# Cached memory keys and values of the sample group as plain fp32 products of 32 columns, with a ring of ten slots

## The chip, the cores and the metric

The kernel runs on one core of one Trainium2 chip. The metric is the device time of one execution in microseconds (us), as the median of several runs. The engines named below are TensorE (PE, with its weight loads PEld), VectorE (DVE), ScalarE (ACT), GpSimd (POOL) and SyncE (SP), which here only issues DMAs.

## The reference, cut to what matters

A two-layer decoder trunk is evaluated for a prompt of 512 tokens and, with the same weights, for a sample group of 8 sequences of 4 tokens. In each layer both groups attend to 256 memory tokens with 4 heads of width 256. The prompt's memory keys and values are computed in the kernel; those of the sample group come from caches, one set for each of its 8 sequences:

```python
def memory_attend(h, mem_k, mem_v, w, layer):
    bsz, seq, _ = h.shape
    q = rms_norm((h @ w['mem_w_q'][layer]).reshape(bsz, seq, MEM_HEADS, MEM_HD), w['mem_q_norm'][layer])
    s = jnp.einsum('blhd,bmhd->bhlm', q, mem_k.astype(q.dtype)).astype(jnp.float32) * MEM_HD ** -0.5
    p = jax.nn.softmax(s, axis=-1).astype(mem_v.dtype)
    o = jnp.einsum('bhlm,bmhd->blhd', p, mem_v).reshape(bsz, seq, D_MODEL)
    return o.astype(h.dtype) @ w['mem_w_o'][layer]
```

For the sample group `mem_k` and `mem_v` are `cache_mem_k[layer]` and `cache_mem_v[layer]`: 8 x 256 x 1024 fp32 numbers each, 8.4 MB each for a layer.

## The kernel before

All matrix products of large size are made in three passes of F32R operands: every operand is split into a high part, rounded to F32R by ACT, and a low part, the remainder, made by DVE, and PE adds up high by high, high by low and low by high (`PASSES`). `projection` (line 100) does so with streamed weights: SP loads chunks of 512 KB, ACT makes `w_high` (line 92), DVE makes `w_low` (line 96), PE multiplies (line 305).

`memory_attention` (line 938) runs once in each of the two layers. It makes the prompt's keys and values, then, in a block called `ring`, loads the first cached keys and clears two buffers `own_high` and `own_low`; then come the query projection (with the weight pair of the output projection loaded at its end), the norm of the queries, the block `attend`, and the output projection. All engines meet at the end of each block.

**The sample group in `attend`.** The caches come as 16 items for a layer: items 0 to 7 are the keys of the eight sequences, items 8 to 15 their values. An item is 1 MB and arrives as two halves of 512 KB, [128, 1024] fp32, in the slots of `ring`, which has 6 (`load`, line 1004). For each half ACT makes `ring_high` (line 1314) and DVE makes `ring_low` (line 1243), in buffers of three slots (`PARTS`). The four query columns of the sequence and of each head lie in `own_high` and `own_low`, which hold zeros elsewhere, so that a window of 128 columns of them puts that sequence and head at its own 4 of 128 output rows; all products of the eight keys add up in one PSUM bank (`half_item`, line 1143). A half item has 4 tiles of three passes, each product 128 x 128 by 128 x 256 (line 1157). After item 7 the scores of all sequences and heads stand in that bank and go through one softmax (stage "sample"), are turned and are used with the values in the same way.

**The prompt in `attend`.** Four heads, each with the stages: `scores` on PE (24 products, line 1113), `shift` on DVE (a maximum and a subtraction over [128, 1024], lines 1205 and 1210), `exps` on ACT (line 1285), `divide` on DVE (a sum, a reciprocal of [128, 4] and a product, lines 1215, 1217 and 1219), `turn` on PE (8 transposes, line 1127), `turned_copy` on ACT (line 1291), `turned_low` on DVE (line 1223), `values` on PE (12 products with 512 columns, line 1138), `high` on ACT (line 1297, two pieces) and `low` on DVE (line 1230, two pieces). `scores` of a head waits for the `shift` of the head before it.

**What sets the order.** Each engine has one stream of instructions, written out by hand. On PE it is: scores 0, item 0, scores 1, item 1, turn 0, item 2, scores 2, values 0, item 3, turn 1, scores 3, values 1, item 4, turn 2, item 5, values 2, item 6, turn 3, item 7, values 3, turn of the sample group, items 8 to 15, and two transposes of the result (line 1190). DVE and ACT have the parts of the items (`low_parts`, `high_parts`) between their softmax steps. SP issues the load of half j once the low part of half j - 6 is made. A half that is not split yet stops PE, and an item that PE has not used yet stops ACT:

```python
act.wait_ge(ring_in[j % RING], 16 * (j // RING + 1))
if j >= PARTS:
    act.wait_ge(used, j - PARTS + 1)
...
pe.wait_ge(split_low, j + 1)
```

**Elsewhere.** The second layer's state-space stage (`s5`, "chunked": the prompt in pieces) has plain fp32 products with a stationary operand of 128 x 32, whose outputs go to 32 PSUM rows each, four in turn (lines 1439 and 1572). The norms use plain fp32 products of 128 x 128 by 128 x 272 (line 389), and the sliding-window attention those of 64 x 128 by 64 x 256 (line 1820). In the profile a plain fp32 product stands as two matmul records, an F32R product as one.

## Time and profile before

| what | value |
|---|---|
| runs | 3186.57, 3183.14, 3183.83 us; median 3183.83 |
| profiled execution | 3189.84 us, of which its span is 3187.9 us |
| PE busy in the span | 2785.0 us (87%) |
| DVE, ACT, POOL busy | 1393.0 us (44%), 964.7 us (30%), 163.2 us (5%) |
| granted TensorE clock, mean | 0.910 |
| DMA | 258.87 MB, mean 81 GB/s |
| loads of `mem_ring` | 64 of 512 KB, median 4.6 us from issue to landing |
| products of line 1157, both layers | 3 kinds x 256, 78.5, 76.4 and 76.2 us busy |
| low parts of the ring (line 1243) | 64, 76.7 us busy on DVE |
| high parts of the ring (line 1314) | 64, 66.6 us busy on ACT |

Busy times of one engine overlap those of others. A matmul's duration is from its start to its modelled end; products that follow each other overlap, so their cost is the distance between starts. The granted clock is given as a share of 2.4 GHz; it has two levels, 1.0 and 0.5 (1.2 GHz), and a mean between them says how long each held. The profiled execution is 6.0 us longer than the median of the runs.

### The profile page before, as it was taken

To read this page: it belongs to the slowest core of one execution; us is meant where nothing else is said; L and a number is where in the kernel's file an instruction comes from. 1 tells how busy PE (TensorE), PEld (TensorE's weight loads), DVE (VectorE), ACT (ScalarE), POOL (GpSimd) and SP (SyncE) were. 2 spreads that over 40 slices of the span, in tenths; PEclk is the share of its full clock that TensorE was granted. 3 is DMA by queue.
4 is the path that set the end of the run, shared out by engine and by line. 5 is a ranking of instruction groups with operands and counts; after the bars stand their busy time and mean duration, and the time that the engine had idled before them with its cause. 6 is when DMAs were issued, how large, how long until landed. Compare 5 with 4: busy or idle time off the path is not lost. (4 is left out here: it accounts for less than half of the span.)

```text
span 3187.9 us, 50690 instructions
## 1 busy us (share of the span) xinstructions
PE 2785.0 (87%) x20835; PEld 2659.6 (83%) x20835; DVE 1393.0 (44%) x1888; ACT 964.7 (30%) x1249; POOL 163.2 (5%) x139
## 2 busy tenths in 40 slices
PE   6999989778586688999989999988698678899998
PEld 6999989757576688999989999986357568899998
DVE  5424433242344554434436334246543547443342
ACT  4412221210434443412224212132432444342221
POOL 0000000000000000000018000050000000000000
PEclk9999999865788899999999999999559889999999
DMA  3222222210133242222222222220103414222222
GB/s 112 96 69 92 94 65 86 81 27 22 49 120 119 66 146 68 90 86 79 89 76 90 93 75 92 73 67 23 38 20 99 139 60 146 77 86 94 73 90 83
DMA packets 76359, 258.87 MB, mean 81 GB/s; under 512 B 9780, under 2 KB 19204, under 8 KB 75232
## 3 DMA queue, kind: packets, MB, share of 16 engines
q1 hardware_dynamic: 75728, 255.81, 24.9%
q0 software_dynamic: 528, 1.64, 0.2%
q8 instruction: 71, 1.16, 0.2%
q14 instruction: 32, 0.26, 0.0%
HBM read 246.85 MB, written 10.57 MB: 81 GB/s over the span
## 5 line engine op out<-in xcount | busy, mean ns | idle before, releaser
L96 DVE TENSOR_TENSOR w_low<-w_raw,w_high 128x1024 fp32r<-128x1024 f32 (+2 forms) x360 | 470.7, 1307 | 1274.6 <-ACT w_high L92 1274.3
L305 PE MATMUL ps<-h_high,w_high 128*128 128x272 f32 x4192 | 887.1, 293 | 124.0 <-DVE h_low L254 67.5
L305 PE MATMUL ps<-h_high,w_low 128*128 128x272 f32 x4192 | 879.1, 292 | 0.0
L305 PE MATMUL ps<-h_low,w_high 128*128 128x272 f32 x4192 | 877.7, 291 | 0.0
L92 ACT ACTIVATE w_high<-w_raw 128x1024 fp32r<-128x1024 f32 (+2 forms) x360 | 399.6, 1111 | 1440.5 <-PE ps L305 1332.9
L305 PEld LDWEIGHTS ps<-h_high,w_high 128*128 128x128 f32 x4192 | 673.4, 192 | 132.0 <-DVE h_low L254 70.5
L305 PEld LDWEIGHTS ps<-h_low,w_high 128*128 128x128 f32 x4192 | 673.0, 193 | 0.0
L305 PEld LDWEIGHTS ps<-h_high,w_low 128*128 128x128 f32 x4192 | 667.2, 192 | 0.0
L305 PE MATMUL ps<-ffn_hid,w_high 128*128 128x272 f32 x2816 | 473.2, 290 | 24.7 <-PEq L149 24.7
L305 PEld LDWEIGHTS ps<-ffn_hid,w_high 128*128 128x128 f32 x2816 | 401.5, 190 | 26.2 <-issue 26.2
L305 PE MATMUL ps<-ffn_hid,w_low 128*128 128x272 f32 x1408 | 294.0, 290 | 0.0
L305 PEld LDWEIGHTS ps<-ffn_hid,w_low 128*128 128x128 f32 x1408 | 222.7, 190 | 0.0
L305 PE MATMUL ps<-mem_mh,w_high 128*128 128x256 f32 x512 | 102.0, 301 | 27.9 <-DVE mem_mh L254 18.1
L305 PEld LDWEIGHTS ps<-mem_mh,w_high 128*128 128x128 f32 x512 | 85.3, 205 | 31.6 <-DVE mem_mh L254 19.1
L1157 PE MATMUL ps<-mem_ring_high,mem_own_high 128*128 128x256 f32 x256 | 78.5, 306 | 22.9 <-DVE mem_ring_low L1243 22.9
L244 DVE SCALAR_TENSOR_TENSOR x<-ps,x 128x544 f32 (+1 forms) x96 | 69.1, 719 | 60.8 <-PE ps L305 60.8
L190 ACT ACTIVATE ffn_up_sg<-ffn_up_sg 128x544 f32<-128x544 f32 x88 | 58.0, 659 | 123.8 <-DVE ffn_up_sg L228 123.8
L1243 DVE TENSOR_TENSOR mem_ring_low<-mem_ring,mem_ring_high 128x1024 fp32r<-128x1024 f32 x64 | 76.7, 1221 | 9.9 <-ACT mem_ring_high L1314 9.5
L1314 ACT ACTIVATE mem_ring_high<-mem_ring 128x1024 fp32r<-128x1024 f32 x64 | 66.6, 1051 | 37.4 <-PE ps L1157 37.4
L1157 PE MATMUL ps<-mem_ring_low,mem_own_high 128*128 128x256 f32 x256 | 76.4, 298 | 0.0
L1157 PE MATMUL ps<-mem_ring_high,mem_own_low 128*128 128x256 f32 x256 | 76.2, 298 | 0.0
L305 PE MATMUL ps<-mem_mh,w_low 128*128 128x256 f32 x256 | 75.5, 295 | 0.0
(379 smaller groups left out, 2476.4 us busy)
## 6 DMA issues: line engine op xcount, KB each, us to landing
w_raw<-in_ffn_w_gate SPq DMA_DIRECT2D x88, 512.0 KB, 3.5
w_raw<-in_ffn_w_up SPq DMA_DIRECT2D x88, 512.0 KB, 3.5
w_raw<-in_ffn_w_down SPq DMA_DIRECT2D x64, 704.0 KB, 4.0
mem_ring<-in_cache_mem_k SPq DMA_DIRECT2D x32, 512.0 KB, 4.6
mem_ring<-in_cache_mem_v SPq DMA_DIRECT2D x32, 512.0 KB, 4.6
w_raw<-in_even_w_in SPq DMA_DIRECT2D x26, 512.0 KB, 3.5
w_raw<-in_mem_w_k SPq DMA_DIRECT2D x16, 512.0 KB, 3.6
w_raw<-in_mem_w_v SPq DMA_DIRECT2D x16, 512.0 KB, 3.5
```

Of the source, the lines that this page charges most:

```text
L92: return nc.scalar.activation(core.high[s][:, 0:kt * P], core.raw[s][:, 0:kt * P], ACT.Copy)
L96: return nc.vector.tensor_tensor(core.low[s][:, 0:kt * P], core.raw[s][:, 0:kt * P], core.high[s][:, 0:kt * P].bitcast(F32), ALU.subtract)
L190: nc.scalar.activation(sg[:], sg[:], ACT.Silu).then_inc(gate_ready, 1)
L244: ins = nc.vector.scalar_tensor_tensor(out, acc[s], scale, out, ALU.mult, ALU.add)
L305: last = nc.tensor.matmul(acc[s][:, a, :], w, x[:, k, a * width:(a + 1) * width], start=(k == 0 and n == 0), stop=(k == kt - 1 and n == 2))
L1157: ins = nc.tensor.matmul(core.ps[:, 6, 0:N_MEM], own[mine][:, i % 2, first:first + P], (ring_high, ring_low)[streamed][:, j % PARTS, at:at ...
L1243: nc.vector.tensor_tensor(ring_low[:, j % PARTS], ring[:, j % RING], ring_high[:, j % PARTS].bitcast(F32), ALU.subtract).then_inc(split_lo ...
L1314: nc.scalar.activation(ring_high[:, j % PARTS], ring[:, j % RING], ACT.Copy).then_inc(split_high, 1)
```

## The change

The sample group's parts are not split any more. An item is 8 plain fp32 products on the fp32 ring itself, each with a stationary operand of 32 columns (the 8 x 4 sample columns of one head, where only the item's own sequence is not zero) and 256 moving columns, and its result goes to the 32 PSUM rows of its head. DVE's and ACT's parts of the items fall away (`low_parts`, `high_parts`), and with them `ring_high`, `ring_low`, `own_high` and `own_low`. In their place are `own_q`, made by one DVE sum of the queries' high and low parts, and `own_p`, made by one ACT copy of the turned probabilities; both are cleared by POOL beforehand, [128, 2048] each.

The ring has 10 slots. Six halves are loaded where six were loaded before; four more are issued by SP in the query projection, behind the first weight chunk that it loads (`fetch`). In `attend` SP issues both halves of item i once PE has used item i - 5. PE waits for the two landings of an item itself, and for `own_q` or `own_p` ahead of item 0 or 8. The order of the steps on PE is as before; line numbers from there on are 2 to 40 less.

```diff
-def projection(nc, core, name, weights, pairs, kt, src, cols, finish, dst, scale=1.0, after=None, norm=None, scaled=False, beside=None):
+def projection(nc, core, name, weights, pairs, kt, src, cols, finish, dst, scale=1.0, after=None, norm=None, scaled=False, beside=None, fetch=None):
...
                 load(0, weights[0][1], kt)
+                if fetch is not None:
+                    fetch(sp)
...
-        RING, PARTS = 6, 3
+        RING, EARLY = 10, 6
         HALF = KT * N_MEM // 2
-        HALVES = 4 * DEC_BATCH
+        ITEMS = 2 * DEC_BATCH
...
-        FRONT = DEC_SEQ * (DEC_BATCH - 1)
-        own = [sb("own_high", [P, 2, FRONT + KT * P], F32R), sb("own_low", [P, 2, FRONT + KT * P], F32R)]
-        zeros = core.mats[:, IDENT, 0:1].unsqueeze(2).broadcast_to([P, 2, FRONT + KT * P])
+        own_q = sb("own_q", [P, KT, DEC_BATCH, TS])
...
         with nc.Block(f"{name}_ring") as block:
             @block.sync
             def _(sp):
-                for j in range(RING):
+                for j in range(EARLY):
                     load(sp, j)
-            @block.scalar
-            def _(act):
-                nc.scalar.activation(own[0][:], zeros, ACT.Copy, scale=0.0)
-            @block.vector
-            def _(dve):
-                nc.vector.tensor_scalar(own[1][:], zeros, 0.0, None, ALU.mult)
+            @block.gpsimd
+            def _(pool):
+                nc.gpsimd.memset(own_q[:], 0.0)
+        def load_more(sp):
+            for j in range(EARLY, RING):
+                load(sp, j)
...
-                   norm=of_x(core, VEC["mem_x_norm"] + KT * layer), scaled=True)
+                   norm=of_x(core, VEC["mem_x_norm"] + KT * layer), scaled=True, fetch=load_more)
...
-        ring_high = sb("ring_high", [P, PARTS, HALF], F32R)
-        ring_low = sb("ring_low", [P, PARTS, HALF], F32R)
+        own_p = sb("own_p", [P, 2, MEM_HEADS, DEC_BATCH, TS])
...
+                @block.gpsimd
+                def _(pool):
+                    nc.gpsimd.memset(own_p[:], 0.0).then_inc(own_cleared, 1)
...
-                    for j in range(RING, HALVES):
-                        sp.wait_ge(split_low, j - RING + 1)
+                    for j in range(RING, 2 * ITEMS):
+                        if j % 2 == 0:
+                            sp.wait_ge(used, (j - RING) // 2 + 1)
                         load(sp, j)
...
-                    def half_item(j):
-                        i, m = j // 2, j % 2
+                    def item(i):
                         b = i % DEC_BATCH
-                        pe.wait_ge(split_low, j + 1)
-                        if i < DEC_BATCH:
-                            tiles = [(h, t, (2 * (h - 2 * m) + t) * N_MEM) for h in (2 * m, 2 * m + 1) for t in range(2)]
-                        else:
-                            tiles = [(h, m, 2 * h * P) for h in range(MEM_HEADS)]
-                        for h, t, at in tiles:
-                            first = FRONT + (2 * h + t) * P - h * TS - b * DEC_SEQ
-                            for n, (mine, streamed) in enumerate(PASSES):
-                                start = b + m + n == 0 and (h, t, at) == tiles[0]
-                                stop = b == DEC_BATCH - 1 and m == 1 and n == 2 and (h, t, at) == tiles[-1]
-                                ins = nc.tensor.matmul(core.ps[:, 6, 0:N_MEM], own[mine][:, i % 2, first:first + P],
-                                                       (ring_high, ring_low)[streamed][:, j % PARTS, at:at + N_MEM],
-                                                       start=start, stop=stop)
+                        for j in (2 * i, 2 * i + 1):
+                            pe.wait_ge(ring_in[j % RING], 16 * (j // RING + 1))
+                        if i == 0:
+                            pe.wait_ge(queries_ready, 1)
+                        elif i == DEC_BATCH:
+                            pe.wait_ge(sample_turned, 1)
+                        for t in range(2):
+                            for h in range(MEM_HEADS):
+                                if i < DEC_BATCH:
+                                    mine = own_q[:, 2 * h + t, b, :]
+                                    part, at = h // 2, (2 * (h % 2) + t) * N_MEM
+                                else:
+                                    mine = own_p[:, t, h, b, :]
+                                    part, at = t, 2 * h * P
+                                ins = nc.tensor.matmul(core.ps[h * TS:(h + 1) * TS, 6, 0:N_MEM], mine,
+                                                       ring[:, (2 * i + part) % RING, at:at + N_MEM],
+                                                       start=(b == 0 and t == 0), stop=(b == DEC_BATCH - 1 and t == 1))
                         ins.then_inc(used, 1)
...
-                    def low_parts(first, count):
-                        for j in range(2 * first, 2 * (first + count)):
-                            i = j // 2
-                            dve.wait_ge(split_high, j + 1)
-                            if j % 2 == 0 and i < DEC_BATCH:
-                                nc.vector.tensor_copy(own_columns(1, i), sample_queries(1, i).bitcast(F32))
-                            elif j % 2 == 0:
-                                nc.vector.tensor_tensor(own_columns(1, i), sample_probs(i),
-                                                        own_columns(0, i).bitcast(F32), ALU.subtract)
-                            nc.vector.tensor_tensor(ring_low[:, j % PARTS], ring[:, j % RING],
-                                                    ring_high[:, j % PARTS].bitcast(F32), ALU.subtract
-                                                    ).then_inc(split_low, 1)
-                    low_parts(0, 1)
+                    sample = [core.h[part][:, :, SEQ:TOK].rearrange("p f (b c) -> p f b c", c=DEC_SEQ) for part in range(2)]
+                    nc.vector.tensor_tensor(own_columns(own_q), sample[0].bitcast(F32), sample[1].bitcast(F32), ALU.add
+                                            ).then_inc(queries_ready, 1)
                     shift(0)
-                    low_parts(1, 1)
...
-                    def high_parts(first, count):
-                        for j in range(2 * first, 2 * (first + count)):
-                            i = j // 2
-                            act.wait_ge(ring_in[j % RING], 16 * (j // RING + 1))
-                            if j >= PARTS:
-                                act.wait_ge(used, j - PARTS + 1)
...
-                            if j % 2 == 0:
-                                source = sample_queries(0, i).bitcast(F32) if i < DEC_BATCH else sample_probs(i)
-                                nc.scalar.activation(own_columns(0, i), source, ACT.Copy)
-                            nc.scalar.activation(ring_high[:, j % PARTS], ring[:, j % RING], ACT.Copy
-                                                 ).then_inc(split_high, 1)
-                    high_parts(0, 1)
-                    high_parts(1, 1)
...
+                    act.wait_ge(turned, NS)
+                    act.wait_ge(own_cleared, 1)
+                    nc.scalar.activation(own_columns(own_p.rearrange("p t h b c -> p (t h) b c")),
+                                         core.ps[:, 7, N_MEM:2 * N_MEM].rearrange("p (f b c) -> p f b c", f=KT, c=DEC_SEQ),
+                                         ACT.Copy).then_inc(sample_turned, 1)
```

PE in `attend`, first layer, at scores 0 and item 0. Before (the last three products of the scores and the first three of the item's 24):

```order
L1113 MATMUL ps<-mem_k_high,h_high 128x256
L1113 MATMUL ps<-mem_k_low,h_high 128x256
L1113 MATMUL ps<-mem_k_high,h_low 128x256
L1157 MATMUL ps<-mem_ring_high,mem_own_high 128x256
L1157 MATMUL ps<-mem_ring_low,mem_own_high 128x256
L1157 MATMUL ps<-mem_ring_high,mem_own_low 128x256
```

After, the same place (the numbers are partitions or columns of the stationary operand by moving columns):

```order
L1108 MATMUL ps<-mem_k_high,h_high 128x256
L1108 MATMUL ps<-mem_k_low,h_high 128x256
L1108 MATMUL ps<-mem_k_high,h_low 128x256
L1155 MATMUL ps<-mem_ring,mem_own_q 32x256 x8
L1108 MATMUL ps<-mem_k_high,h_high 128x256
```

The item's 24 products became 8, between the same scores.

DVE at the start of `attend`, first layer. Before:

```order
L1239 CAST mem_own_low<-h_low 128x8x4
L1243 TENSOR_TENSOR mem_ring_low<-mem_ring,mem_ring_high 128x1024 x2
L1205 TENSOR_REDUCE rstd<-ps 128x4
L1210 TENSOR_TENSOR mem_prob<-ps,rstd 128x1024
L1239 CAST mem_own_low<-h_low 128x8x4
L1243 TENSOR_TENSOR mem_ring_low<-mem_ring,mem_ring_high 128x1024 x2
L1215 TENSOR_REDUCE rstd<-mem_prob 128x4
```

After:

```order
L1233 TENSOR_TENSOR mem_own_q<-h_high,h_low 128x8x8x4
L1203 TENSOR_REDUCE rstd<-ps 128x4
L1208 TENSOR_TENSOR mem_prob<-ps,rstd 128x1024
L1213 TENSOR_REDUCE rstd<-mem_prob 128x4
L1215 RECIPROCAL rstd<-rstd 128x4
L1217 TENSOR_TENSOR mem_prob<-mem_prob,rstd 128x1024
L1203 TENSOR_REDUCE rstd<-ps 128x4
```

The softmax steps now follow each other on DVE; ACT has lost its parts in the same way.

SP from the block `ring` into the query projection, first layer (the weights of the query projection are `mem_w_q`). Before:

```order
L1009 DMA mem_ring<-in_cache_mem_k 128x1024 x6
L1018 UNCONDITIONAL_BRANCH
L150 UNCONDITIONAL_BRANCH
L153 DMA w_raw<-in_mem_w_q 128x1024
L157 UNCONDITIONAL_BRANCH
L157 ISA
```

After:

```order
L1011 DMA mem_ring<-in_cache_mem_k 128x1024 x6
L1024 UNCONDITIONAL_BRANCH
L150 UNCONDITIONAL_BRANCH
L153 DMA w_raw<-in_mem_w_q 128x1024
L1011 DMA mem_ring<-in_cache_mem_k 128x1024 x4
L159 UNCONDITIONAL_BRANCH
```

Four loads moved from `attend` to the query projection, ahead of the weight chunks that follow the first.

## Rows read from the trace of the kernel before

**Rows 1.** Stretches of both attend blocks: us, busy by engine, PEclk, DMA share, GB/s.

```profile
1077.30:1146.20 68.90, 55.45 (x370) 51.22 (x370) 51.75 (x64) 32.25 (x47) 0.00 (x0) 0.92 0.38 122
1146.20:1171.20 25.00, 24.94 (x192) 24.63 (x192) 18.88 (x22) 15.15 (x20) 0.00 (x0) 0.93 0.63 211
...
2610.80:2679.80 69.00, 56.34 (x370) 52.51 (x370) 51.79 (x64) 32.37 (x47) 0.00 (x0) 0.90 0.38 122
2679.80:2706.00 26.20, 26.10 (x192) 25.75 (x192) 18.89 (x23) 15.12 (x20) 0.00 (x0) 0.88 0.60 201
```

**Rows 2.** Groups by line, first attend block: count | busy us, mean ns | idle before.

```profile
L1243 DVE TENSOR_TENSOR mem_ring_low<-mem_ring,mem_ring_high 128x1024 fp32r<-128x1024 f32 x32 | 38.4, 1221 | 5.5 <-ACT mem_ring_high L1314 5.2
...
L1314 ACT ACTIVATE mem_ring_high<-mem_ring 128x1024 fp32r<-128x1024 f32 x32 | 33.3, 1051 | 19.2 <-PE ps L1157 19.2
...
L1230 DVE TENSOR_TENSOR h_low<-ps,h_high 128x512 fp32r<-128x512 f32 x8 | 5.2, 684 | 0.4 <-ACT h_high L1297 0.4
...
L1205 DVE TENSOR_REDUCE rstd<-ps 128x4 f32<-128x1024 f32 x4 | 4.9, 1224 | 4.5 <-PE ps L1113 4.5
...
L1297 ACT ACTIVATE h_high<-ps 128x512 fp32r<-128x512 f32 x8 | 4.4, 587 | 0.9 <-PE ps L1138 0.8
L1285 ACT ACTIVATE mem_prob<-mem_prob 128x1024 f32<-128x1024 f32 x4 | 4.2, 1058 | 16.4 <-DVE mem_prob L1210 16.4
...
L1217 DVE RECIPROCAL rstd<-rstd 128x4 f32<-128x4 f32 x4 | 0.7, 178 | 0.1
```

**Rows 3.** PE's timeline in the first attend block: start, us, line, count, [idle before].

```profile
1082.21 0.28 PE L1157 MATMUL ps<-mem_ring_high,mem_own_high 128*128 128x256 f32 x1
...
1095.80 0.58 PE L1157 MATMUL ps<-mem_ring_high,mem_own_high 128*128 128x256 f32 x1 [4.01 <-DVE mem_ring_low L1243]
...
1100.07 0.28 PE L1113 MATMUL ps<-mem_k_high,h_high 128*128 128x256 f32 x1
...
1102.92 0.40 PE L1138 MATMUL ps<-mem_pT_high,mem_v_high 128*128 128x512 f32 x1
...
1105.48 0.40 PE L1138 MATMUL ps<-mem_pT_high,mem_v_low 128*128 128x512 f32 x1
1106.87 0.39 PE L1157 MATMUL ps<-mem_ring_high,mem_own_high 128*128 128x256 f32 x1 [0.99 <-DVE mem_ring_low L1243]
...
1109.83 1.04 PE L1127 MATMUL ps<-mats,mem_prob 128*128 128x128 f32 x8
```

**Rows 4.** PE's timeline in the state-space stage, around line 1572.

```profile
2174.75 0.42 PE L1563 MATMUL ps<-odd_proj,s_near 128*128 128x136 f32 x1
2175.10 2.07 PE L1572 MATMUL ps<-s_before,s_ca 128*32 128x136 f32 x64
```

**Rows 5.** The same stretch, line 1572 alone: us, PE busy, PEld busy, PEclk.

```profile
2175.10:2177.50 2.40, 2.07 (x64) 1.78 (x64) 1.00 0.00 0
```

**Rows 6.** Plain fp32 products elsewhere: line 389 (ns min/median/max, first to last start), and 1820.

```profile
L389 PE MATMUL ps<-mem0qn_sq,mats x32: 392/393/497, 1052.3 to 1059.8; 128*128 128x272 f32 x32
...
2346.79 1.22 PE L1820 MATMUL ps<-odd_proj 64*128 64x256 f32 x2
```

**Rows 7.** The first six ring loads: ns of an issue, first to last issue, time to landing.

```profile
L1009 SPq DMA_DIRECT2D mem_ring<-in_cache_mem_k x6: 340/456/634, 986.6 to 989.2; - x6
...
DMA to landing us min/median/max: 4.1/6.6/8.6
```

**Rows 8.** A stretch among the items of values, columns as in Rows 1.

```profile
1150.00:1160.00 10.00, 10.00 (x84) 9.92 (x84) 8.31 (x10) 7.17 (x12) 0.00 (x0) 1.00 0.88 292
```

**Rows 9.** Two weight chunks behind the ring loads, and ACT's first use of the second.

```profile
L153 SPq DMA_DIRECT2D w_raw<-in_mem_w_q x2: 327/334/342, 990.2 to 997.0; - x2
...
DMA to landing us min/median/max: 4.4/6.7/8.9
...
1011.11 2.21 ACT L92 ACTIVATE w_high<-w_raw 128x1024 fp32r<-128x1024 f32 x2
```

**Rows 10.** POOL's groups by line: its only clearing of this size.

```profile
L1465 POOL MEMSET s_near<- 128x2048 f32 x1 | 1.8, 1814 | 328.1 <-POOLq L72 328.1
```

More of the change, by code:

```diff
@@ L1160, in half_item @@
                         ins.then_inc(used, 1)
                     def items(first, count):
-                        for j in range(2 * first, 2 * (first + count)):
-                            half_item(j)
+                        for i in range(first, first + count):
+                            item(i)
                     scores(0)
```

44 lines of the change are left out of this document (9 added, 35 removed).

## The prediction, made before the changed kernel had run

> **What bounds the kernel now.** I read the stage table first. In the two `attend` blocks [rows 1] the first part (the prompt's four heads, with items 0 to 7 between them) takes 68.9 and 69.0 us with PE busy 55.5 of 68.9 and DVE 51.8; the second (items 8 to 15) takes 25.0 and 26.2 us with PE busy throughout. So the first blocks end 93.9 us and the second 95.2 us after they start, 189.1 us in all, of the profiled 3187.9. Next the groups by line [rows 2]: splitting the ring costs DVE 38.4 us and ACT 33.3 us for each block, and DVE has these parts between the steps of the softmax. Last, PE's timeline [rows 3]: it stood 4.01 and 0.99 us ahead of items, both times for `ring_low`. The first part is thus a chain in which the softmax waits behind splits on DVE, and PE behind both; the second is PE's own time. An item costs PE 2.96 us: its first product starts at 1106.87, the transposes behind it at 1109.83.
>
> **Removed: the splits and two thirds of the products.** DVE loses 32 x 1.22 us, ACT 32 x 1.05 us for each block [rows 2], besides the small parts of `own`. That is worth only what the chain of the softmax then allows, so the block is walked through below.
>
> **Added: eight plain fp32 products of 32 columns for an item.** The nearest row is the state-space stage's line 1572: the same form, 128 x 32, four outputs to four groups of PSUM rows in turn. Its 32 products of 136 columns (64 records) take 2.07 us with their tail, at a granted clock of 1.00 [rows 4, 5]. A record outlasts the start of the next by its tail: for the F32R products 0.28 us of duration against 2.85/24 = 0.12 between starts [rows 3], 0.16 us. That leaves 1.91 us, 60 ns a product. The other bound is the norm's line 389, plain fp32 with all 128 columns and no neighbour to run beside: 32 records of 272 columns start within 7.5 us, 0.242 us each, two to a product [rows 6], so 0.484 x 256/272 = 0.455 us for a product of 256 columns. By line 1572 an item is 8 x 60 ns x 256/136 = 0.90 us, by line 389 it is 3.64 us. I take 0.90: form, order of the groups and operand type are those of line 1572; 3.64 is a rival.
>
> A switch between the full array and 32 columns comes with each item among the heads. In the trace line 1572 starts at 2175.10, before the modelled end of the full product ahead of it (2174.75 + 0.42) [rows 4]: no gap. The Trainium skill (TensorEngine Tiling (Array Packing), Tiling Modes) says the opposite, that a change of the tiling mode drains the engine. By it each of 18 switches in a block would cost up to one product's length, 0.42 us, so at most 7.6 us a block and 15 us in all, and 3134 us in place of the forecast; the row speaks against it.
>
> **Walk through the block after the change,** from its start, with durations of [rows 2, 3]. A DVE pass over 1024 columns is 1.22 us (five of them per head, lines 1205, 1210, 1215, 1219, 1223), an ACT pass 1.06.
> 1. Scores 0 run at the lower clock as before and end at 4.9 us (item 0 started at 1082.21).
> 2. Head 0: shift 2 x 1.22, exp 1.06, divide 2 x 1.22 + 0.18: 6.1 us, to 11.0. Head 1 the same, to 17.2; its neighbour's `turned_low` 1.22, to 18.4.
> 3. Heads 2 and 3: 6.1, plus `low` of the head before (2 x 0.68) and `turned_low` 1.22: 8.7 us each, to 35.8. PE's work for a head, scores 2.85 (1100.07 to 1102.92), values 2.8 (twelve, 0.233 apart from 1102.92), turn 1.04, two items 1.8, is 8.5 us and lies under this DVE chain, as do `high` (0.59 each) and the sum that makes `own_q`.
> 4. Values 2 on PE 2.8, item 6 0.90, turn 3 1.04, ACT copy 1.06, `turned_low` 1.22: 42.8. Values 3: 45.6; the sample group's softmax (256 columns) lies beside them. Its two transposes, a quarter of 1.04, and the ACT copy into `own_p` (256 columns, at most 0.59): 46.5.
> 5. Items 8 to 12 are in the ring by then (the last loaded after item 7, at 41.5): 5 x 0.90, to 51.0.
> 6. Items 13 to 15 load when items 8, 9 and 10 are used, from 47.4 on. Six halves issued from 986.6 to 989.2 landed from 4.1 us after the first issue to 8.6 us after the last [rows 7]: 990.7 to 997.8, 1.42 us for each further half, 369 GB/s. Pair 13 is in at 47.4 + 4.1 + 1.42 = 52.9, pair 14 at 55.8, pair 15 at 58.6; with item 15 the end is 59.5.
>
> So transfers set the last 8 us, not PE. The saving is 93.9 - 59.5 = 34.4 and 95.2 - 59.5 = 35.7: 70 us. Against it stands the clock. After standing 4.01 us PE took 4.27 us for an item (1095.80 to 1100.07) in place of 2.96 [rows 3]: 1.3 us for a dip. PE will stand oftener, up to 3 us behind DVE and 2 us for each late pair, and the output projection then starts at the lower level. I allow two dips on the path of each block: 5 us. **Sum: 65 us less.**
>
> **What moves.** Four loads go ahead of the later query weights on SP's queue. Before, the two chunks behind the ring loads landed 8.9 and 4.4 us after their issues at 990.2 and 997.0, so at 999.1 and 1001.4; ACT first splits the second in the pair of passes that starts at 1011.11 [rows 9]. Four halves more put it 4 x 1.42 = 5.7 us later at most, to 1007.1: still 4 us early, cost nothing; with that cover gone, up to 5.7 us a layer. SP's issues, 0.46 us each [rows 7], delay only that chunk, which waits for its buffer anyway. The clearing in the block `ring` moves to POOL: 1.8 us for 2048 columns [rows 10] beside SP's six issues (986.6 to 989.2 and on), so nothing; the second one lies under the first scores. PE's new waits for landings have all later PE work queued behind them, but only items 13 to 15 meet one: nothing else is late by the walk.
>
> **Rivals.**
> - *The four groups of columns run one after another.* An item is 3.64 us [rows 6]. PE then has 4 x 6.7 + 2 (the slow start) for the heads and 8 x 3.64 in the first part, 58 us, and 29 in the second: 87. The saving is 15 us: 3169. For it: nothing but caution; against it line 1572 [rows 4].
> - *PE stays at the lower clock through the block.* The dips of before, 0.92 and 0.90 in the first parts [rows 1], become the rule because an item's burst is short. PE's first part doubles, 2 x (26.8 + 7.2) = 68 and some 4 exposed, then 8 items of 1.8, partly behind transfers: 84. The saving is 21 us: 3163. The Trainium skill describes this (TensorE: Matmul & The Clock Gate, HAM oscillation): bursts that are short against their waits for DMA run cold each time. Against it: heads keep PE busy about 8.5 of 8.7 us by step 3.
> - *Slower: each product waits for the end of the one before,* because two records and a load of weights stand for each. Line 1820, 64 x 128 by 256 columns alone, took 1.22 us from the start of its first record to the end of its second [rows 6]. At even half of that an item is 4.9 us, the first part 28.8 + 39 = 68, the second 39: 107, 25 us lost in all: 3209. It decides from 0.51 us for a product (16 items of 4.07 + 28.8 = 94). Line 1572's 64 records in 2.07 us speak against it.
> - *Loads no faster than among the items now,* 292 GB/s [rows 8]: 3.6 us a pair in place of 2.84, 2.3 us a block: 3124. It is in the range.
>
> **How the numbers follow.** The profiled execution took 3189.8 us, 6.0 more than the median; both should move alike. 3189.8 - 65 = 3125 for a profiled one, 3183.8 - 65 = **3119** for the median. The range: without dips 3114, with 5 us for quicker items or landings 3108; upwards slower loads 5, the uncovered weight chunk 11, four more dips 5, part of the switches 7: 3147. Chances: forecast 0.81, groups in series 0.05, low clock 0.07, slower 0.04, the rest 0.03 spread. A measurement can tell 0.2% (6 us) from no change; both lesser gains are over it. Faster 0.93, same 0.02, slower 0.05.
>
> **What would show it.** Right: `attend` about 61 us in both layers; line 1155's 16 records of an item within 0.9 us at full clock; DVE in step 3 without a wait but for exp; three PE waits for ring landings at the end, about 2 us each, and none before; query projection unchanged. Wrong: records of line 1155 at 0.2 us or more from each other; a PE clock of 0.5 through the heads; waits for `mem_ring` among items 0 to 12; ACT waiting for `w_raw` in the query projection.

## The result, and the profile after

The changed kernel takes 3131.24 us (median of four runs, 3128.77 to 3136.26) beside 3185.2 us for the kernel before (four runs, 3183.14 to 3192.88): 54 us less by the medians, and a ratio of the means of 0.9828 with a 95% interval of 0.9807 to 0.9849. It is faster by a little under 2%, and inside the range, but 12 us above the 3119 that was forecast. The profiled execution took 3128.77 us with a span of 3127.0, which is 60.9 us shorter than the span of before; it is the fastest of the four runs, and the profiled execution of before (3189.84) lies above the median of its runs, so the spans are further apart than the medians.

The first view answers [rows 1]: the two `attend` blocks cut at the start of item 8 and the end of item 15. Columns are the stretch and its length, busy us (instructions) of PE, PEld, DVE, ACT and POOL, the mean granted clock, the busy share of the DMA engines, GB/s.

```profile
1073.60:1120.90 47.30, 38.54 (x310) 29.29 (x314) 31.74 (x38) 13.25 (x18) 1.78 (x1) 0.96 0.54 174
1120.80:1137.50 16.70, 10.33 (x128) 5.07 (x128) 0.35 (x1) 0.00 (x0) 0.00 (x0) 0.74 0.60 201
2579.70:2626.60 46.90, 38.09 (x310) 28.83 (x311) 31.70 (x38) 13.26 (x18) 1.75 (x1) 0.97 0.53 174
2626.50:2643.20 16.70, 10.32 (x128) 5.06 (x128) 0.44 (x2) 0.00 (x0) 0.00 (x0) 0.73 0.60 207
```

The part with the heads went from 68.9 and 69.0 us to 47.2 and 46.9, the items behind it from 25 and 26 to 16.6 and 16.5. In the second part PE is now busy 10.3 of 16.7 us, where it was busy throughout before. From the first scores to the end of item 15 a block takes 63.9 and 63.4 us (93.8 and 95.1 before): 61.7 us less for both. Three small things make the difference to the span: the steps between item 15 and the output projection, 0.2 us longer; the two output projections, 1.2 and 2.5 us longer; and 3.2 us less elsewhere, most of it ahead of the first block, which starts at 1073.6 instead of 1077.4. The kernels run below with the same instructions ahead of it start it anywhere from 1073.4 to 1080.5, so this is not the change's doing. What the change did is 61.7 - 0.2 - 3.7, some 58 us.

The products of an item among the heads, line 1155, and PE's timeline around two of them (start, us, line, count):

```profile
L1155 PE MATMUL ps<-mem_ring,mem_own_q x16: 379/379/404, 1078.4 to 1079.1; 128*32 128x256 f32 x16
...
1083.93 0.27 PE L1108 MATMUL ps<-mem_k_high,h_low 128*128 128x256 f32 x1
1084.13 1.07 PE L1155 MATMUL ps<-mem_ring,mem_own_q 128*32 128x256 f32 x16
1085.13 1.09 PE L1122 MATMUL ps<-mats,mem_prob 128*128 128x128 f32 x8
1086.16 1.07 PE L1155 MATMUL ps<-mem_ring,mem_own_q 128*32 128x256 f32 x16
```

The 16 records of an item start within 0.7 us, in fours 0.216 us apart. The item takes 1.07 us with its tail, and 1.00 us from its start to that of the transposes behind it, where it took 2.96 [rows 3]. Each group starts before the modelled end of the one ahead, though the engine changes between the full array and 32 columns each time. The change is not free even so: the item starts 0.20 us after the score product ahead of it (1083.93 to 1084.13), where those products follow each other at 0.12.

The end of the first block on PE's timeline, with the wait ahead in brackets, and the six loads of the items waited for (ns of an issue, first to last issue; us to landing):

```profile
1120.84 4.52 PE L1155 MATMUL ps<-mem_ring,mem_own_p 128*32 128x256 f32 x80 [0.83 <-ACT mem_own_p L1294]
1130.43 1.94 PE L1155 MATMUL ps<-mem_ring,mem_own_p 128*32 128x256 f32 x16 [5.06 <-DMA mem_ring<-in_cache_mem_v]
1133.02 1.93 PE L1155 MATMUL ps<-mem_ring,mem_own_p 128*32 128x256 f32 x16 [0.65 <-DMA mem_ring<-in_cache_mem_v]
1135.53 1.93 PE L1155 MATMUL ps<-mem_ring,mem_own_p 128*32 128x256 f32 x16 [0.57 <-DMA mem_ring<-in_cache_mem_v]
1138.00 0.69 PE L1188 MATMUL ps<-mats,mem_prob 128*128 128x128 f32 x2 [0.54 <-DVE mem_prob L1254]
...
L1011 SPq DMA_DIRECT2D mem_ring<-in_cache_mem_v x6: 327/432/1057, 1122.0 to 1124.7; - x6
...
DMA to landing us min/median/max: 3.6/8.7/10.7
```

Items 8 to 12 run through in 4.52 us, and 13 to 15 wait for the ring. The first of the six halves lands 3.6 us after its issue (1125.6) and the second only at 1130.3, 4.7 us behind it; the other four follow at 1.25 us each, to 1135.4. While PE stood the granted clock fell from 1.00 to 0.50 (2.4 to 1.2 GHz), so the three late items take 1.93 us each. The output projection, too, begins at that level (0.51 in its first 6.2 us), where before it had 0.70 in the first 5.7 (and 1.00 in the second layer):

```profile
1127.50:1130.00 2.50, 0.00 (x0) 0.00 (x0) 0.00 (x0) 0.00 (x0) 0.00 (x0) 0.77 0.88 282
1130.00:1132.50 2.50, 1.94 (x16) 0.69 (x16) 0.00 (x0) 0.00 (x0) 0.00 (x0) 0.50 0.95 390
...
1139.80:1146.00 6.20, 6.12 (x27) 6.15 (x28) 1.23 (x1) 1.06 (x1) 0.00 (x0) 0.51 0.56 172
```

### The profile page after: what moved, and what is told of

Read it like the earlier page. It is cut to its first block and busy times, and to the rows that moved or that the text cites. A ratio compares the mean times of both kernels' runs of the same rounds, so it can differ in the third digit from the quotient of the medians.

```text
span 3127.0 us, 49964 instructions
## 1 busy us (share of the span) xinstructions
PE 2722.8 (87%) x20579; PEld 2579.9 (83%) x20579; DVE 1314.5 (42%) x1792; ACT 892.9 (29%) x1151; POOL 171.7 (5%) x143
## 5 line engine op out<-in xcount | busy, mean ns | idle before, releaser
L246 DVE SCALAR_TENSOR_TENSOR x<-ps,x 128x544 f32 (+1 forms) x96 | 69.0, 719 | 60.9 <-PE ps L307 60.9
L242 DVE TENSOR_TENSOR ffn_hid<-ffn_up_prod,ffn_hid 128x544 f32 (+1 forms) x88 | 68.2, 775 | 10.1
L230 DVE TENSOR_TENSOR ffn_up_up<-ps,rstd 128x544 f32<-128x544 f32 x88 | 63.3, 719 | 18.1 <-PE ps L307 18.1
L236 DVE TENSOR_TENSOR ffn_up_prod<-ffn_up_sg,ffn_up_up 128x544 f32<-128x544 f32 x88 | 64.7, 735 | 3.0
L230 DVE TENSOR_TENSOR ffn_up_sg<-ps,rstd 128x544 f32<-128x544 f32 x88 | 63.2, 719 | 0.0
L256 DVE SCALAR_TENSOR_TENSOR h_low<-x,vectors,h_high 128x544 fp32r<-128x544 f32 x64 | 53.6, 896 | 18.0 <-ACT h_high L196 18.0
```

What stands on the lines that cost most here:

```text
L230: nc.vector.tensor_tensor(in_groups(to[:], cols), acc[s], in_groups(rstd, cols), ALU.mult).then_inc((gate_scaled, up_scaled)[s], 1)
L236: nc.vector.tensor_tensor(prod[:], sg[:], up[:], ALU.mult).then_inc(product_ready, 1)
L242: nc.vector.tensor_tensor(low, prod[:], high.bitcast(F32), ALU.subtract).then_inc(hid_ready, 1)
L246: ins = nc.vector.scalar_tensor_tensor(out, acc[s], scale, out, ALU.mult, ALU.add)
L256: nc.vector.scalar_tensor_tensor(src[1][:, k], x_tiles[k], core.vec(gain + k), src[0][:, k].bitcast(F32), ALU.mult, ALU.subtract).then_inc ...
```

## The experiments

"Block" is always from the first scores to the end of item 15, in the first and the second layer. Edits are to the changed kernel unless said otherwise. A time is that of one execution, but for `ring14`, `warm` and `pool_queue`, which ran four times each; the rows are the surer evidence. The kernel before stood at 3187.38 us beside `hfirst`, `ring6`, `ring14` and `warm`, at 3195.98 beside `one_group`, `splits_kept`, `splits_out` and `act_tail`, and at 3192.03 beside `keys_twice` and `pool_queue`.

**Where the gain comes from: splits or products.** Two kernels take the change apart, each from its own side.

`splits_kept`: the new products, with every split of the ring done again and used by nobody; a load waits for the split of its slot as before.

```diff
+ sp.wait_ge(split_low, j - RING + 1)
...
+ nc.scalar.activation(ring_high[j % 3], ring[:, j % RING], ACT.Copy).then_inc(split_high, 1)
...
+ nc.vector.tensor_tensor(ring_low, ring[:, j % RING], ring_high[j % 3].bitcast(F32), ALU.subtract
+                         ).then_inc(split_low, 1)
```

> The changed kernel's products, and DVE's and ACT's splits of every half of the ring kept as dead work in the places they have in the kernel before; a load waits for the split of its slot as before. Theory (the walk of the prediction): the softmax of the heads is one chain through DVE, and 32 passes of 1.22 us among its steps lengthen it, so item 8 starts not at 47 us but near 62 to 66, and the block takes about 82 us: more than half of the 30 us that the change saves is the splits. Rival: the 16 products of an item that went were what PE gated the block by; then the kept splits lie beside PE and the block stays near 64 us.

`splits_out`, an edit to the kernel before: its 24 F32R products and its ring of six, without splits from the fourth half on (the products read again what the first three left).

```diff
- sp.wait_ge(split_low, j - RING + 1)
+ sp.wait_ge(used, j - RING + 1)
...
+ if j >= PARTS:
+     continue
```

> The kernel before with its 24 F32R products for an item, its ring of six and its issue order, but the splits only of the first three halves: the later ones multiply the parts that those left, so the sample group's output is not the reference's. Theory: DVE's chain is shorter, but PE still spends 2.96 us on an item, so the heads' part is PE's (4 heads of 6.7 us and 8 items of 2.96, with the slow start) and the eight items behind take 24 us: the block takes 75 to 78 us instead of 93.8, so the splits alone are worth some 17 us a layer and the products the remaining 13. Rival: products alone gave the gain; then the block stays within 3 us of 93.8.

Their stretches in the first block, `splits_kept` first (to item 8 and to the end of item 15 in both):

```profile
1076.00:1136.90 60.90, 43.24 (x309) 32.66 (x311) 50.67 (x54) 28.77 (x35) 0.00 (x0) 0.82 0.41 134
1136.90:1154.10 17.20, 10.31 (x128) 5.09 (x128) 15.42 (x14) 14.52 (x15) 0.00 (x0) 0.74 0.59 199
```

```profile
1075.30:1127.50 52.20, 51.38 (x370) 48.91 (x371) 35.20 (x42) 16.43 (x23) 0.00 (x0) 0.95 0.49 158
1127.50:1150.50 23.00, 22.92 (x192) 22.74 (x192) 0.34 (x2) 0.00 (x0) 0.00 (x0) 1.00 0.68 237
```

`splits_kept` took 3174.55 us, blocks 78.0 and 76.8; the remaining splits then hold the block's last transposes back to 83.6 us after its start (64.4 in the changed kernel). `splits_out` took 3150.13 us, blocks 75.1 and 75.5. The two agree: the splits are worth 18.7 us of the first block (93.8 to 75.1) or 19.2 (83.6 to 64.4), products and ring together the other 11.3 (75.1 to 63.9) or 10.7 (94.3, where the last transposes stood before, to 83.6). Neither alone is the gain, and the heads' part is a little shorter than expected with the splits kept (item 8 at 60.9 us, the end of item 15 at 78 instead of 82). With the splits kept, PE stands (43 of 60.9 us busy, clock 0.82) behind a DVE that is busy 50.7; with the old products, PE is busy 51.4 of 52.2 us and sets the pace itself. Both rivals fall.

**What makes the products cheap.** `one_group` sends all products to the same 32 rows of PSUM (and starts and ends the sum accordingly); `hfirst` changes the order, so that the two products for the same rows follow each other.

```diff
- ins = nc.tensor.matmul(core.ps[h * TS:(h + 1) * TS, 6, 0:N_MEM], mine,
+ ins = nc.tensor.matmul(core.ps[0:TS, 6, 0:N_MEM], mine,
...
- start=(b == 0 and t == 0), stop=(b == DEC_BATCH - 1 and t == 1))
+ start=(b == 0 and t == 0 and h == 0), stop=(b == DEC_BATCH - 1 and t == 1 and h == 3))
```

> All eight products of an item write the same 32 rows of PSUM, so that the output of the sample group is not the reference's; loads, waits, bytes and the number of products are those of the changed kernel. My theory: the four groups of 32 columns take their products side by side, four in 0.216 us, and that alone gives the 1.07 us of an item; in one group the 16 records follow each other, 0.216 us from start to start, so an item takes about 3.5 us and a block, with PE then as the bound, about 87 us (23 us more than after's 63.6). Rival: products of 32 columns are short in any place, because the columns that PE loads as weights are few; then records stay four within 20 ns, an item stays near 1.1 us and the block at 63 to 64 us.

```diff
- for t in range(2):
-     for h in range(MEM_HEADS):
+ for h in range(MEM_HEADS):
+     for t in range(2):
```

> The changed kernel with the two loops of an item swapped: the two products of a head now follow each other, so neighbours go to the same 32 PSUM rows; the work is the same. Theory (four groups of columns run side by side, a product of 256 columns taking some 0.44 us in its own group): each product waits for its neighbour of the same head, five such steps make an item 2.1 to 2.3 us in place of 1.07, and an attend block grows from 63.6 to about 70 us; the run comes out 10 to 14 us above the changed kernel. Rival (an item is bound by the issue of its 16 records, whatever rows they go to): an item stays at 1.07 us and the time within 3 us of the changed kernel.

Line 1155 in one item of `one_group`, and its two stretches in the first block; then the same item in `hfirst`:

```profile
L1155 PE MATMUL ps<-mem_ring,mem_own_q x16: 379/379/479, 1078.8 to 1082.1; 128*32 128x256 f32 x16
...
1073.40:1133.00 59.60, 58.78 (x306) 39.65 (x307) 32.12 (x38) 13.35 (x18) 1.78 (x1) 0.95 0.43 138
1133.00:1160.90 27.90, 27.79 (x128) 13.99 (x128) 0.38 (x2) 0.00 (x0) 0.00 (x0) 1.00 0.36 121
```

```profile
L1155 PE MATMUL ps<-mem_ring,mem_own_q x16: 379/379/404, 1080.8 to 1081.5; 128*32 128x256 f32 x16
```

In one group the records start 0.216 us apart, an item takes 3.64 us, PE is busy throughout, the blocks take 87.4 and 86.9 us and the kernel 3176.44. A record is as long as before (379 ns), so products of 32 columns are not short in themselves: four run side by side when they go to four groups of rows. That is 23.5 us of each block. `hfirst` went against its expectation: 1.09 us for an item, 3129.33 us, blocks 63.1 and 67.9 (the second with its item 8 at 51.8 us, 4.9 later than in the changed kernel, before any of its loads is waited for: the granted clock was 0.50 twice among its heads, from 2595.8 to 2599.1 and from 2612.9 to 2619.5). The groups need not alternate: in this order, too, four records start within 0.04 us of each other and the next four 0.2 us behind them.

**What sets the end: the ring and its transfers.** `ring6` gives the changed kernel the old six slots, `ring14` fourteen (one of them a weight buffer that stands idle in the block, and `own_p` put into `own_q`).

```diff
- RING, EARLY = 10, 6
+ RING, EARLY = 6, 6
```

> The changed kernel with a ring of 6 slots and no early loads, so a pair of halves waits for the item three before it. Theory (splits and products made the gain, the ring only shortens the tail): by the walk the block ends 5.6 us later than with ten slots, 69 us where 63.6 was measured, and the run is 11 to 13 us above the changed kernel, still some 45 us under the kernel before. Rival (the ring carries the gain): the block is back over 80 us.

```diff
- RING, EARLY = 10, 6
+ RING, EARLY, OWN = 14, 6, 10
...
+ more = [core.raw[0][:, 0:HALF]]
...
+ more.extend(sb(f"slot{r}", [P, HALF])[:] for r in range(RING - OWN - 1))
```

> The changed kernel with 14 slots: one in a weight buffer that stands empty during attend, three where own_p was and beside it; own_p shares own_q's place. Loads of items 5 and 6 start with the block, and only item 15 waits for a load released among the values (by item 8). Theory (in the changed kernel the last three items wait for transfers, and PE then runs them and the start of the output projection at the lower clock): the block ends near 55 us in place of 63.6, items 13 and 14 take 0.9 us each, PE keeps the full clock into the output projection, and the run comes out near 3109 (18 to 24 us under the changed kernel). Rival (the tail is short of something else, or landings simply move): within 6 us of the changed kernel.

PE's end of the first block in `ring14`:

```profile
1125.11 3.66 PE L1156 MATMUL ps<-mem_ring,mem_own_q 128*32 128x256 f32 x64 [0.83 <-ACT mem_own_q L1294]
...
1130.28 1.07 PE L1156 MATMUL ps<-mem_ring,mem_own_q 128*32 128x256 f32 x16
1132.39 1.07 PE L1156 MATMUL ps<-mem_ring,mem_own_q 128*32 128x256 f32 x16 [1.04 <-DMA mem_ring<-in_cache_mem_v]
```

And a stretch among its heads, at values 2 (columns as in the first view):

```profile
1112.00:1115.30 3.30, 3.22 (x8) 2.55 (x9) 0.02 (x1) 0.26 (x1) 0.00 (x0) 0.50 0.89 297
```

`ring6` took 3140.03 us, blocks 67.2 and 68.7: the ring's four more slots are worth 3.3 and 5.3 us, so that the products have 7 to 8 us of the first block's 11. The time is 8.8 us above the changed kernel's, a little less than the 11 to 13 expected. `ring14` took 3111.64 us (3108.91 to 3120.15; ratio 0.9749, interval 0.9722 to 0.9776), blocks 57.7 and 56.7: one item still waits, 1.04 and 0.29 us, the clock holds at the end, and both projections take 49.9 us. It beats both kernels, though its profiled execution is the slowest of its four (3120.15). Its blocks miss the expected 55 because the heads take some 2 us longer (item 8 at 49.3 and 49.1 us): in the first layer the scores at the start took 5.46 us instead of 4.89 and values 2 took 4.52 instead of 3.01, after PE had stood 2.46 us for DVE. What differs is the granted clock: 0.50 at values 2 here, in the line above and in the second layer too, and 1.00 in the changed kernel, behind the same wait (2.46 us). Why it fell in the one and held in the other, these runs do not show.

**What the low clock costs.** `warm` fills the waits ahead of items 13 to 15 with 30, 8 and 8 products that nobody reads.

```diff
+ WARM = {13: 30, 14: 8, 15: 8}
...
+ for n in range(WARM[i]):
+     nc.tensor.matmul(core.ps[:, 0, 0:N_MEM], v_part[0][:, 0, 0, :], k_part[0][:, 0, :], start=True, stop=True)
```

> The changed kernel with extra products that nobody reads, 30 F32R products of 128 x 256 ahead of item 13 and 8 each ahead of items 14 and 15, in the time in which PE waits for the loads. Theory (the waits let the clock fall to the lower level, which costs 1 us in each of the last three items and about 3 us at the start of each output projection): the granted clock stays at 1.0 through the tail, the late items take 1.07 us each, the block is about as long (62 to 64 us) and the output projection starts at full clock; 5 to 8 us less than the changed kernel. Rival (the clock at that place costs nothing, since the projection waits for weights or splits there): within 2 us of the changed kernel, or slower by what the extra products delay the late items.

```profile
1136.63 1.07 PE L1156 MATMUL ps<-mem_ring,mem_own_p 128*32 128x256 f32 x16 [0.56 <-DMA mem_ring<-in_cache_mem_v]
...
1139.78 1.07 PE L1156 MATMUL ps<-mem_ring,mem_own_p 128*32 128x256 f32 x16 [0.93 <-DMA mem_ring<-in_cache_mem_v]
...
1142.28 1.07 PE L1156 MATMUL ps<-mem_ring,mem_own_p 128*32 128x256 f32 x16 [0.29 <-DMA mem_ring<-in_cache_mem_v]
```

3128.06 us (3123.73 to 3131.91; ratio 0.9799, interval 0.9771 to 0.9827): 3 us under the changed kernel by the medians, while the intervals overlap. The rows show it more surely: late items take 1.07 instead of 1.93 us and the projections 49.9 instead of 51.1 and 50.9. The blocks, 62.9 and 63.8, gain little, because the items still wait for landings. From the start of item 8 to the end they gain 1.0 and 1.6 us, but in the second block 1.9 are lost among the heads, where the clock fell to 0.50 as in `ring14`. So the filling brought less than the 5 to 8 us expected. It does not give back all that the clock costs, either: the projections still begin at 0.70 in their first 5.7 us, and one that begins at 1.00 takes 48.3 us (both in `splits_out` and in `pool_queue`).

**Why one transfer lands late.** In the changed kernel the halves of a pair land 1.25 us apart as a rule. One half lands 4.7 us behind its neighbour at the first block's end (3.6 in the second, and the next 2.3), and ahead of that pairs 10 and 12 land 2.8 to 3.4 us behind the pair ahead of them. Three kernels look for the cause: `act_tail` issues the second halves of the last three pairs on ACT's queue, `keys_twice` reads the keys again in place of the values, and `pool_queue` issues every later second half on POOL's queue.

```diff
- load(sp, j)
+ if not (j >= 26 and j % 2):
+     load(sp, j)
...
+ for i in range(13, ITEMS):
+     act.wait_ge(used, i - 4)
+     load(act, 2 * i + 1)
```

> The changed kernel with the second halves of items 13, 14 and 15 issued on ACT's queue beside the first halves on SP's. If the one late landing (the second half of pair 13 lands 8 us after its issue, 4.7 us after the first half) comes from SP's queue, which moves one transfer behind the other, the second halves land with the first and item 15 ends some 3 us earlier: a block of 60 to 61 us. If it comes from the memory side or the 16 DMA engines that both queues share, the same stretch stalls again and the block takes 63 to 64 us.

```diff
- a["cache_mem_v"][layer, i - DEC_BATCH].rearrange("p t f c -> p (t f c)"))
+ a["cache_mem_k"][layer, i - DEC_BATCH].rearrange("p k c -> p (k c)"))
```

> The changed kernel, but the eight loads of the cached values read the cached keys again (same size and shape), so the sample group's output is not the reference's. The late landings in the changed kernel (a load that lands 3.3 to 4.7 us after the one ahead of it, where 1.25 us is the rule) are all among the values. If the place in memory makes them late, they vanish here: from the start of item 8 to the end of item 15 some 13 us instead of 16.5, a block of about 60 us. If it is the queue and the moments of the issues, the same loads land late again and the block takes 63 to 64 us.

```diff
+ for j in range(RING + 1, 2 * ITEMS, 2):
+     pool.wait_ge(used, (j - RING) // 2 + 1)
+     load(pool, j)
...
- for j in range(RING, 2 * ITEMS):
+ for j in range(RING, 2 * ITEMS, 2):
```

> The changed kernel with the second half of every pair from the eleventh load on issued on POOL's queue, beside the first half on SP's. If the late landings belong to one queue, as two queues in the tail alone suggest (13.2 and 13.6 us from item 8 to the end of item 15, where the changed kernel takes 16.6 and 16.5), they shrink here for pairs 10 and 12 too, and from item 8 to the end of item 15 it is again about 13 us: blocks of 60 to 61 us and 3122 to 3126 us. If POOL's issues are themselves slower than SP's (nothing in these traces shows their cost), pairs land later than in the changed kernel and the blocks take 64 us or more.

Items 8 to 15 of the first block on PE's timeline, `act_tail` first, then `keys_twice`, then `pool_queue`:

```profile
1123.12 4.52 PE L1156 MATMUL ps<-mem_ring,mem_own_p 128*32 128x256 f32 x80 [0.83 <-ACT mem_own_p L1295]
1129.35 1.07 PE L1156 MATMUL ps<-mem_ring,mem_own_p 128*32 128x256 f32 x16 [1.71 <-DMA mem_ring<-in_cache_mem_v]
1132.42 1.07 PE L1156 MATMUL ps<-mem_ring,mem_own_p 128*32 128x256 f32 x16 [2.00 <-DMA mem_ring<-in_cache_mem_v]
1134.41 1.94 PE L1156 MATMUL ps<-mem_ring,mem_own_p 128*32 128x256 f32 x16 [0.92 <-DMA mem_ring<-in_cache_mem_v]
```

```profile
1130.01 1.07 PE L1155 MATMUL ps<-mem_ring,mem_own_p 128*32 128x256 f32 x16 [1.89 <-DMA mem_ring<-in_cache_mem_k]
1133.42 1.20 PE L1155 MATMUL ps<-mem_ring,mem_own_p 128*32 128x256 f32 x16 [2.34 <-DMA mem_ring<-in_cache_mem_k]
1135.92 1.94 PE L1155 MATMUL ps<-mem_ring,mem_own_p 128*32 128x256 f32 x16 [1.30 <-DMA mem_ring<-in_cache_mem_k]
```

```profile
1134.50 1.07 PE L1164 MATMUL ps<-mem_ring,mem_own_p 128*32 128x256 f32 x16 [2.18 <-DMA mem_ring<-in_cache_mem_v]
1138.23 3.91 PE L1164 MATMUL ps<-mem_ring,mem_own_p 128*32 128x256 f32 x32 [2.65 <-DMA mem_ring<-in_cache_mem_v]
```

From the start of item 8 to the end of item 15, both layers: 16.6 and 16.5 us in the changed kernel, 13.2 and 13.6 in `act_tail` (3125.28 us, blocks 62.5 and 60.4), 14.3 and 16.0 in `keys_twice` (3126.91; 63.3 and 62.8), 14.3 and 14.3 in `pool_queue` (3131.64, 3125.47 to 3134.54, ratio 0.981 with interval 0.9775 to 0.9844; 61.6 and 61.5). Over the whole kernel `pool_queue` is no faster than the changed kernel, although in the profiled execution its blocks and projections are 9 us shorter together: other stretches are longer, 6.9 us of it ahead of the first block, which starts at 1080.5. That is why the comparison goes by stretches and not by the time.

The last six loads of `act_tail` in the first block (ns of an issue, first to last issue; us to landing), and what the DMA engines did meanwhile:

```profile
L1011 SPq DMA_DIRECT2D mem_ring<-in_cache_mem_v x3: 328/328/329, 1124.2 to 1126.0; - x3
L1011 ACTq DMA_DIRECT2D mem_ring<-in_cache_mem_v x3: 361/362/391, 1124.2 to 1126.0; - x3
...
DMA to landing us min/median/max: 4.5/6.8/8.3
...
1127.50:1130.00 2.50, 0.79 (x17) 0.50 (x16) 0.00 (x0) 0.00 (x0) 0.00 (x0) 1.00 1.01 405
1130.00:1132.50 2.50, 0.49 (x12) 0.11 (x8) 0.00 (x0) 0.00 (x0) 0.00 (x0) 1.00 1.03 419
```

At the block's end two queues take the late landing away. In `act_tail` the two halves of a pair land 0.2 to 0.7 us apart and the pairs 1.8 to 2.5 us behind each other, which is the regular pace of two halves; the last six landings lie within 5.5 and 5.4 us of each other, where they take 9.8 and 9.6 in the changed kernel and 7.1 to 9.9 in the other kernels with ten slots, the cheap products and one queue (`hfirst`, `warm`, `keys_twice`). In `pool_queue` they take 6.9 and 6.7. Ahead of the end two queues do not help: with every pair on two queues, pairs 10 and 12 of the first layer still land 2.9 and 3.1 us behind the pair ahead of them (3.4 us both, on one queue). So SP's queue alone is not the cause, and `pool_queue` falls short of the 13 us expected of it. The Trainium skill (DMA: Bandwidth & Descriptors, Issuing engines are not separate DMA queues) says that transfers of all issuing engines share the same 16 engines and interleave, so that a second issuer saves issue time alone. Pairs 10 and 12 agree with that. The blocks' ends do not: in `act_tail` the six issues start within 1.7 us in both blocks, where they take 2.8 and 3.1 in the changed kernel, so 1.0 and 1.4 us are saved there, while the last landing comes 10.0 and 10.4 us behind the first issue instead of 13.4 and 13.3. `keys_twice` rules out the values' place in memory: pairs 10 and 12 are as late (3.2 and 3.4 us), and at the two ends one landing comes 2.2 and 4.3 us behind its neighbour. In the changed kernel the single packets of those 4.7 us are uneven: their median is 159 to 227 ns in each half microsecond, but the longest take up to 2.0 us, while in the regular stretch behind none takes over 159 ns. What holds them up was not settled.

## Why the prediction was right, and by how much off

- **Item of 0.90 us, by line 1572 [rows 4, 5]: right.** Items 8 to 12 run at 0.86 us each (80 records in 4.52 with one tail). The rival's price from line 389 [rows 6] was right as well: 3.64 us for groups in series, a block of 87, is what `one_group` measured.
- **No gap at a switch of the tiling: right for the sum, not for the reading.** In the rows above transposes start at 1085.13, 0.07 us before the item ahead ends (1084.13 + 1.07), and line 1572 did the same in [rows 4] (2174.75 + 0.42 against 2175.10). Products that follow each other without a switch overlap by more, 0.16 us by the prediction's own working. A score product is followed by an item after 0.20 us instead of 0.12, and the transposes by an item after 0.20 instead of 0.03 before. So a switch costs 0.1 to 0.2 us, not 0.42; for the 18 switches of a block that is an estimate of some 2 us of PE's time, all among the heads, where DVE sets the pace. The Trainium skill (TensorEngine Tiling (Array Packing), Tiling Modes) has a drain there. The trace fits a short one, and the 15 us priced by that rule did not come.
- **Steps 1 to 5: right.** Item 8 was forecast at 46.5 us and came at 47.2 and 46.9; item 12's end at 51.0, and came at 51.8 and 51.4. No item up to 12 waited for the ring, and POOL's clearing and the sum that makes `own_q` delayed none. In step 3 of the first block DVE waited for the exponentials alone, 1.12 us for a head, as forecast; its waits for scores (4.51 us) and for `high` (3.7 us) lie in steps 1 and 4.

```profile
1078.55 1.22 DVE L1203 TENSOR_REDUCE rstd<-ps 128x4 f32<-128x1024 f32 x1 [4.51 <-PE ps L1108]
...
1095.70 1.22 DVE L1213 TENSOR_REDUCE rstd<-mem_prob 128x4 f32<-128x1024 f32 x1 [1.12 <-ACT mem_prob L1264]
...
1111.64 0.69 DVE L1228 TENSOR_TENSOR h_low<-ps,h_high 128x512 fp32r<-128x512 f32 x1 [2.38 <-ACT h_high L1276]
```

- **Step 6, transfers: the term that was mis-sized.** Forecast were 11.2 us from the first issue to the last landing, at 1.42 a half [rows 7]; it took 13.4 and 13.3. The regular pace was better, 1.25 us, but one landing came late by 3.4 us (in the second block two did, by as much together). In the first block the end at 63.85 us instead of 59.5 is made of 1.0 us (issue at 48.4 instead of 47.4), 2.2 us (transfers) and 1.2 us (the last item and its start took 2.06 instead of 0.90, at the lower clock). The forecast of three waits of 2 us became one of 5.06 and two of 0.6. The prediction took a mean pace from a burst into an empty ring [rows 7] and had no term for a half that lands late.
- **The clock: the right size, in part by luck.** 5 us were allowed for two dips on the path of each block, whether among the heads, at the late pairs or at the projection's start. In the profiled execution the heads show none after the start. The last items lost 0.86 us in each block (1.93 instead of 1.07) and the projections 1.2 and 2.5: 5.4 us. Other executions with the same heads came out otherwise. In 6 of 16 blocks (of the changed kernel, `hfirst`, `ring6`, `ring14`, `warm`, `act_tail`, `keys_twice` and `pool_queue`) the clock fell to 0.50 among the heads, and item 8 came some 2 us later, once 4.9; and several of these projections began at a higher clock. So the sum of 5 us holds for the profiled execution, and not as a property of the kernel. The rival of a low clock through the block did not come, only that of its end, from 1129 to 1146 us in the first layer.
- **Priced at nothing: the earlier loads and POOL's clearing.** The second chunk of weights was issued at 993.1 and landed at 1002.6, and ACT took the two chunks' pair up at 1007.4 without a wait for it. The clearings (1.8 us each) stood in nobody's way.

```profile
L153 SPq DMA_DIRECT2D w_raw<-in_mem_w_q x2: 328/336/343, 986.5 to 993.1; - x2
...
DMA to landing us min/median/max: 9.0/9.2/9.4
...
1007.37 2.08 ACT L92 ACTIVATE w_high<-w_raw 128x1024 fp32r<-128x1024 f32 x2
```

The walk gave 70.1 us and the two blocks 61.7. The missing 8.4 are the two ends: 4.3 of transfers, 1.6 of later issues, 2.3 of the last item, of which the clock has 1.7. With the projections' 3.7 the clock took 5.4, which the allowance covers; so the two ends without the clock, 6.7 us, are what the forecast lacked, and some 58 us are left of the forecast 65. The medians say 54; the 4 us between are within what runs of one kernel differ by (3128.8 to 3136.3).

## What to carry to other kernels

When a change takes two engines' work away at once, take it apart from both sides: here each part alone leaves the other engine as the bound, and what each is worth could be read only with the other held. Where the end of a stage hangs on the last few transfers, price them by the spread of landings in the trace and not by their mean pace, and try more slots first: each four slots of this ring gave 3 to 7 us a block. Narrow products pay when they go to different groups of rows of PSUM; the order among them did not matter. And where the clock fell in some executions and held in others, as among the heads here, compare stretches of several traces before a cost of 2 us is put down to an edit.

## What the runs showed of the hardware

Four plain fp32 products of 128 x 32 by 256 columns to four groups of PSUM rows start together, four records in 0.216 us, and in one group one record in 0.216 us; two products in a row for the same group do not hold back the others (`hfirst`, 1.09 us an item against 1.07). After PE had stood 5 us, three bursts of 16 records with pauses of 0.6 us between them all ran at 0.50, and the clock came back only some 6 us into the dense projection; with the wait filled by products nobody reads, the same items took 1.07 us. A projection of 384 products takes 48.3 us when it begins at 1.00, 49.9 when the clock is 0.70 in its first 5.7 us, and 51.1 and 50.9 when it is 0.50. Between the full array and 32 columns the next product starts some 0.07 us before the modelled end of the one ahead, where neighbours without such a change overlap by 0.16. Of 512 KB transfers issued close together most land 1.25 us apart, but in each of the eight block ends with ten slots, side-by-side products and one queue (the changed kernel, `hfirst`, `warm`, `keys_twice`) at least one of the last six landings came 2.2 to 4.7 us behind its neighbour, from either place in memory. With the pairs of the end on two queues (`act_tail`, `pool_queue`, four ends) the last six landed within 5.4 to 6.9 us instead of 7.1 to 9.9. In `ring6`, where slots come free one pair at a time, the last five gaps were 1.1 to 1.8 us.
